# A decoder trunk's middle: combining expert outputs, norm, turn and value products in one loop over token tiles

## The reference

```python
h = h + s5_mixer(rmsnorm(h, norm_mix[0]), ...)          # layer 0
h = h + hier_moe(rmsnorm(h, norm_ffn[0]), ...)          # 2 of 32 experts for each token
# in hier_moe, last step: out[tok] += gate_k * y[tok, k] for k = 0, 1
k, v = split(rmsnorm(h, norm_kv) @ w_kv + b_kv)         # 256 + 256 columns
q = rmsnorm(h, norm_mix[1]) @ w_q + b_q                 # 1024 columns
h = h + attention(q, k, v) @ w_o + b_o                  # window 128, meta tokens, sinks
h = h + hier_moe(rmsnorm(h, norm_ffn[1]), ...)          # layer 1
out = rmsnorm(h, norm_final)[:, 16:]
# rmsnorm(x, g) = x / sqrt(mean(x * x) + 1e-6) * g
```

## Time and profile before

| | us |
|---|---|
| median of 3 runs | 2242.67 (2241.44 to 2243.80) |
| the profiled execution: its own time | 2243.16 |
| its span, first to last instruction | 2241.4 |
| PE busy / DVE / ACT / POOL in the span | 1985.4 / 1586.7 / 1244.6 / 369.5 |
| mean granted TensorE clock | 0.941 of full speed |

### The profile page before, as it was taken

The page is one execution under the profiler, slowest core; times in us unless marked ns, Lnnn a source line. Parts: engine busy times, 40 slices in busy tenths (PEclk is TensorE's granted clock), DMA queues, the critical chain, the costliest instruction groups (busy, mean ns, idle before and its releaser), DMA issues. The chain is left out here.

```text
span 2241.4 us, 31742 instructions
## 1 busy us (share of the span) xinstructions
PE 1985.4 (89%) x10658; PEld 1572.3 (70%) x10658; DVE 1586.7 (71%) x1770; ACT 1244.6 (56%) x1521; POOL 369.5 (16%) x684
## 2 busy tenths in 40 slices
PE   4859999659999999999189999998599999999991
PEld 3558777548888888887178766666388888888880
DVE  8995221558888888887642276663688888888885
ACT  6524110437777777776120065554277777777772
POOL 2000000302211112221224000002022212112214
PEclk9979999879999999999579999999699999999995
DMA  3265100639999999996521020005299999999985
GB/s 98 36 60 176 63 1 1 248 113 365 381 375 371 367 373 374 377 376 253 189 67 38 10 86 1 1 1 198 103 343 360 360 375 385 378 384 387 383 315 235
DMA packets 136045, 504.69 MB, mean 225 GB/s; under 512 B 38466, under 2 KB 68498, under 8 KB 84754
## 3 DMA queue, kind: packets, MB, share of 16 engines
q1 hardware_dynamic: 116258, 468.85, 57.4%
q0 software_dynamic: 18432, 33.86, 4.0%
q10 hardware_dynamic: 1280, 0.98, 0.3%
HBM read 488.47 MB, written 47.32 MB: 239 GB/s over the span
## 5 line engine op out<-in xcount | busy, mean ns | idle before, releaser
L1406 DVE TENSOR_TENSOR moe_lo<-moe_raw,moe_hi 128x2048 fp32r<-128x2048 f32 x378 | 861.0, 2292 | 118.4 <-ACT moe_hi L1191 114.1
L1191 ACT CAST moe_hi<-moe_raw 128x2048 fp32r<-128x2048 f32 x374 | 714.2, 1915 | 153.5 <-PE moe_ps_g L1546 74.9
L1544 PE MATMUL moe_ps_g<-moe_hi,moe_x_hi 128*128 128x512 f32 x512 | 211.6, 413 | 7.2 <-DVE moe_x_lo L1411 4.7
L1544 PE MATMUL moe_ps_y<-moe_hi,moe_h_hi 128*128 128x512 f32 x512 | 209.0, 408 | 3.7 <-DVE moe_h_lo L1422 3.7
L1545 PE MATMUL moe_ps_g<-moe_hi,moe_x_lo 128*128 128x512 f32 x512 | 205.8, 402 | 0.0
L1546 PE MATMUL moe_ps_g<-moe_lo,moe_x_hi 128*128 128x512 f32 x512 | 205.3, 401 | 0.0
L1545 PE MATMUL moe_ps_y<-moe_hi,moe_h_lo 128*128 128x512 f32 x512 | 204.2, 399 | 0.0
L1546 PE MATMUL moe_ps_y<-moe_lo,moe_h_hi 128*128 128x512 f32 x512 | 203.9, 398 | 0.0
L1546 PE MATMUL moe_ps_u<-moe_lo,moe_x_hi 128*128 128x512 f32 x512 | 203.0, 396 | 0.0
L1544 PE MATMUL moe_ps_u<-moe_hi,moe_x_hi 128*128 128x512 f32 x512 | 202.8, 396 | 0.0
L1545 PE MATMUL moe_ps_u<-moe_hi,moe_x_lo 128*128 128x512 f32 x512 | 202.8, 396 | 0.0
(11 more groups left out here) (406 smaller groups left out, 3699.1 us busy)
## 6 DMA issues: line engine op xcount, KB each, us to landing
moe_raw<-moe_w_gate SPq DMA_DIRECT2D x128, 1024.0 KB, 7.3
moe_raw<-moe_w_up SPq DMA_DIRECT2D x128, 1024.0 KB, 8.0
moe_raw<-moe_w_down SPq DMA_DIRECT2D x128, 1024.0 KB, 7.3
moe_raw<-y_dram SPq DMA_DIRECT2D x16, 1024.0 KB, 11.6
mix_r<-ssm_w_glu SPq DMA_DIRECT2D x16, 512.0 KB, 5.2
xn_dram<-moe_work SPq DMA_DIRECT2D x16, 512.0 KB, 7.4
mix_r<-x SPq DMA_DIRECT2D x8, 512.0 KB, 5.4
mix_r<-h_dram SPq DMA_DIRECT2D x16, 256.0 KB, 11.6
```

Source lines behind the costliest of these rows:

```text
L1191: A.copy(hi[:, slot(number, k), :], raw[:, k, :]).then_inc(hi_done, 1)
L1406: V.tensor_tensor(lo[:, slot, :], raw[:, k, :], hi[:, slot, :].bitcast(F32), ALU.subtract).then_inc(lo_done, 1)
L1544: T.matmul(out, x_h, w_h, start=first, stop=False)
```

## The change

**In `phase_moe`, layer 0.** The tiles' loads and the combine leave the phase, but for the first four loads (`load_pair`), which SyncE still issues at its end. They go to a buffer `yc` of its own with four places, which lies over the expert phase's `hi` and the first slot of `lo`. The order of tiles is now `TILE_ORDER`: the meta tile first, then 0 to 7. The four K/V weight blocks are loaded here, as soon as `raw` slot 3 of the last expert has been split, into `w_raw` (over `raw` slots 2 and 3); block numbers 0 and 1 are now V, 2 and 3 K. VectorE multiplies them by the gain and later subtracts the `hi` part in place (`w_lo` has the address of `w_raw`); ScalarE makes the `hi` parts (`w_hi`, over `raw` slots 4 and 5) ahead of the last `store_y`.

**In `phase_project`.** One loop over the tiles does everything up to V. On VectorE, trip j combines tile j, writes 1/rms of tile j-1 onto a diagonal (`prj_scale` = identity times the column `rstd`), takes the `lo` part of tile j-2 and the V result of tile j-3. TensorE's `turn` multiplies the tile itself by that diagonal (float32 `matmul`), which normalises and turns at once, so `prj_xn` is gone; behind `turn(j)` stands the V product of tile j-1. K and Q blocks follow as before, with four weight slots in place of three and two; a Q block is loaded when the products of the block four before it are done. The three bias loads and the Q gain are issued by ScalarE at the head of its list. Ahead of the first turn, TensorE multiplies the identity by itself 20 times.

```diff
+W_KV = 4
+N_YC = 4
+RAW_AT = 229344 - 6 * 8192
+TILE_ORDER = (XT,) + tuple(range(XT))
...
+def kv_columns(t, n):
+
+    half = DC // W_KV
+    at = (n + half) % W_KV * P
+    return t["w_kv"].rearrange("(p c) f -> p c f", c=DC)[:, :, at:at + P]
...
+def load_pair(sp, t, j):
+
+    i = TILE_ORDER[j]
+    n = tile_rows(i)
+    sp.dma_start(t["yc"][0:n, j % N_YC],
+                 t["y_dram0"][2 * i * P:2 * (i * P + n), :].rearrange("(p k) d -> p k d", k=2)
+                 ).then_inc(t["yc_in"][j % N_YC], 16)
...
+            else:
+
+                sp.dma_start(g_kv[:, :], t["norm_kv"].rearrange("(p c) -> p c", c=DC)).then_inc(wkv_in, 16)
+                sp.wait_ge(lo_done, n_q * 6 + (-2))
+                for n in range(W_KV):
+                    sp.dma_start(t["w_raw"][:, n], kv_columns(t, n)).then_inc(wkv_in, 16)
...
-            for i in range(NT):
+            if not last_layer:
+                for j in range(N_YC):
+                    load_pair(sp, t, j)
+            for i in range(NT if last_layer else 0):
                 if i >= NB:
                     sp.wait_ge(h_new, 2 * (i - NB + 1))
...
             store_y(n_q - 2, n_q * 6)
+            if not last_layer:
+                for n in range(W_KV):
+                    act.wait_ge(gained, n + 1)
+                    A.copy(t["w_hi"][:, n], t["w_raw"][:, n]).then_inc(wkv_hi, 1)
             store_y(n_q - 1, n_q * 6 + 2)
...
+            if not last_layer:
+                dve.wait_ge(wkv_in, 16 * (W_KV + 1))
+                for n in range(W_KV):
+                    V.tensor_tensor(t["w_raw"][:, n], t["w_raw"][:, n], g_kv[:, :].unsqueeze(2).to_broadcast([P, DC, P]),
+                                    ALU.mult).then_inc(gained, 1)
+                for n in range(W_KV):
+                    dve.wait_ge(wkv_hi, n + 1)
+                    V.tensor_tensor(t["w_lo"][:, n], t["w_raw"][:, n], t["w_hi"][:, n].bitcast(F32),
+                                    ALU.subtract).then_inc(wkv_lo, 1)
...
+                    load_pair(sp, t, j)
+            for i in range(NT if last_layer else 0):
...
+            for j in range(N_YC, NT):
+                sp.wait_ge(h_new, 2 * (j - N_YC + 1))
+                load_pair(sp, t, j)
...
+            for n in range(Q0, NC):
+                sp.wait_ge(acc_done, jobs_to(n - W_KV))
+                sp.dma_start(w_raw[:, n % W_KV], w_q[:, :, (n - Q0) * P:(n - Q0 + 1) * P]).then_inc(w_in[n % W_KV], 16)
...
+            for j, i in enumerate(TILE_ORDER):
...
+            pool.wait_ge(gain_in, 16)
             pool.wait_ge(bo_in, 16)
-            pool.wait_ge(xn_done, NT)
-            for n in range(3, NP):
-                gain(n)
-                if n >= V_P:
-                    i = n - V_P
-                    nc.gpsimd.tensor_tensor(h[:, i, :], h[:, i, :], sq[:, :], ALU.add).then_inc(bo_added, 1)
...
+            A = nc.scalar
+            A.dma_start(bv[:, :], t["b_kv"][KV:].partition_broadcast(P)).then_inc(bias_in, 16)
+            A.dma_start(bk[:, :], t["b_kv"][0:KV].rearrange("(c p) -> p c", p=P),
+                        allow_slow_non_contiguous=True).then_inc(bias_in, 16)
+            A.dma_start(bq[:, :], t["b_q"][0].rearrange("(c p) -> p c", p=P),
+                        allow_slow_non_contiguous=True).then_inc(bias_in, 16)
+            A.dma_start(g_q[:, :], t["norm_mix"][1].rearrange("(p c) -> p c", c=DC)).then_inc(gain_in, 16)
...
+            for j in range(NT):
+                squares(j)
+                if j >= 1:
+                    hi_part(j - 1)
+            hi_part(NT - 1)
...
+            def combine(j):
+                i = TILE_ORDER[j]
+                n = tile_rows(i)
+                dve.wait_ge(yc_in[j % N_YC], 16 * (j // N_YC + 1))
+                for k in range(2):
+                    V.scalar_tensor_tensor(h[0:n, i, :], yc[0:n, j % N_YC, k, :], gates[0:n, k, i:i + 1],
+                                           h[0:n, i, :], ALU.mult, ALU.add).then_inc(h_new, 1)
+                    dve.wait_ge(h_new, 2 * j + k + 1)
+
+            def set_scale(j):
+                i = TILE_ORDER[j]
+                n = tile_rows(i)
+                dve.wait_ge(rstd_done, j + 1)
+                if j >= 2:
+                    dve.wait_ge(xt_mm, j - 1)
+                V.tensor_scalar(scale[0:n, j % 2, 0:n], ident[0:n, 0:n], rstd[0:n, i:i + 1], None,
+                                ALU.mult).then_inc(scale_set, 1)
...
+            for j in range(NT + 3):
+                if j < NT:
+                    combine(j)
+                if 1 <= j <= NT:
+                    set_scale(j - 1)
+                if 2 <= j <= NT + 1:
+                    lo_part(j - 2)
+                if j == 3:
+                    dve.wait_ge(bias_in, 48)
+                if j >= 3:
+                    values(j - 3)
+            k = NT
...
+            def turn(j):
+                i = TILE_ORDER[j]
+                n = tile_rows(i)
+                pe.wait_ge(scale_set, j + 1)
+                if j >= 2:
+                    pe.wait_ge(xt_lo, j - 1)
+                for c in range(DC):
+                    last = T.matmul(ps_x[:, j % 2, c * P:c * P + n],
+                                    h[0:n, i, :].rearrange("p (m c) -> p c m", c=DC)[:, c, :],
+                                    scale[0:n, j % 2, 0:n], start=True, stop=True)
+                last.then_inc(xt_mm, 1)
+
...
+            def value_product(j):
+                pe.wait_ge(xt_lo, j + 1)
+                i = TILE_ORDER[j]
+                product(j, 0, i * P, tile_rows(i))
             pe.wait_ge(ident_step, 2)
+            for _ in range(20):
+                T.matmul(acc[:, 3, 0:P], ident[:], ident[:], start=True, stop=True)
+            for j in range(NT):
+                turn(j)
+                if j >= 1:
+                    value_product(j - 1)
...
-                pe.wait_ge(xn_done, i + 1)
-                if i >= 2:
-                    pe.wait_ge(xt_lo, i - 1)
-                for c in range(DC):
-                    last = T.transpose(ps_x[:, i % 2, c * P:c * P + n],
-                                       xn[0:n, i % 2, :].rearrange("p (m c) -> p c m", c=DC)[:, c, :],
-                                       ident[0:n, 0:n])
-                last.then_inc(xt_mm, 1)
```

More of the change, by code:

```diff
@@ L871, in phase_moe @@
         sem = semaphore_source(nc, ctx, f"moe{layer}_")
+        hi, lo = (sb(x, [P, 3, KC * F], F32R) for x in ("hi", "lo"))
         ident = sb("ident", [P, P])
@@ L919, in phase_moe @@
         n_more = sb("n_more", [1, 1], I32)
-        raw = sb("raw", [P, 6, KC * F])
-        hi, lo = (sb(x, [P, 3, KC * F], F32R) for x in ("hi", "lo"))
+        raw = nc.alloc_sbuf_tensor_at(f"moe{layer}_raw", [P, 6, KC * F], F32, offset=RAW_AT)
+        g_kv = sb("g_kv", [P, DC])
         gi = sb("gi", [P, 1], I32)
@@ L954, in phase_moe @@
                              "ht_mm", "ht_hi", "ht_lo", "y_done", "y_out"))
-        yc_in = [sem(f"yc_in{b}") for b in range(NB)]
+        if last_layer:
+            yc_in = [sem(f"yc_in{b}") for b in range(NB)]
+        wkv_in, gained, wkv_hi, wkv_lo = (sem(x) for x in ("wkv_in", "gained", "wkv_hi", "wkv_lo"))
         y_free, h_new, fin_sq, fin_rstd, fin_done, out_done = (
@@ L1659, in jobs, with jobs_to @@
         def jobs(n):
-            if n < K_P:
+            if n < K0:
+                return [(i * P, tile_rows(i)) for i in TILE_ORDER] if n == K0 - 1 else []
+            if n < Q0:
                 return [(0, 512), (512, 512), (XT * P, N_META)]
-            if n < V_P:
-                return [(i * P, tile_rows(i)) for i in range(NT)] if n == V_P - 1 else []
             return [(0, 512), (512, 512)]
-        def jobs_before(n):
-            return sum(len(jobs(m)) for m in range(n))
+        def jobs_to(n):
+            return sum(len(jobs(m)) for m in range(max(n + 1, K0)))
         block = ctx.enter_context(nc.Block())
@@ new lines, in hi_part @@
+            def hi_part(j):
+                i = TILE_ORDER[j]
+                n = tile_rows(i)
+                act.wait_ge(xt_mm, j + 1)
+                A.copy(x_hi[:, :, i * P:i * P + n],
+                       ps_x[:, j % 2, :].rearrange("p (c m) -> p c m", c=DC)[:, :, 0:n]).then_inc(xt_hi, 1)
+            for j in range(NT):
[3 more added lines that the diff above has]
+            hi_part(NT - 1)
+            for n in range(Q0, NC):
+                act.wait_ge(gained, n - Q0 + 1)
+                A.copy(w_hi[:, n % W_KV], w_raw[:, n % W_KV]).then_inc(w_hi_done, 1)
@@ L1787, in _ @@
-            k = 0
-            for n in range(NP):
-                ahead = n + 1 < NP and n != V_P - 1
-                if ahead:
+            dve.wait_ge(ident_step, 2)
+            for j in range(NT + 3):
[9 more added lines that the diff above has]
+                    values(j - 3)
@@ L1791, in _ @@
+            k = NT
+            for n in range(K0, NC):
+                if Q0 <= n + 1 < NC:
                     split_w(n + 1)
@@ new lines, in product @@
+            def product(k, n, at, m):
```

(26 more changed lines are left out.)

164 lines of the change are left out of this document (51 added, 113 removed).

## The result

The changed kernel takes 2214.56 us (median of 4 runs, 2213.56 to 2215.1), the kernel before beside it 2243.24 (2241.44 to 2245.32): ratio 0.9871, 95% interval 0.9857 to 0.9885. The direction was right; the gain is 28.7 us where 43.7 were forecast, and the time lies 1.6 us above the range. The profiled execution took 2213.56 us, its span is 2211.8.

A forecast was written before the change was run, and what follows sets the result against it. It took the combine as bound by VectorE, the norm part by a chain through four engines, the products by TensorE. Phase start 1073.8 + 53.2 to the last V + 27.6 K + 89.1 Q = 1243.7, before 1287.3: 2199.5 us, range 2190 to 2213.

The forecast's parts named there:

- the full turn: Loop over tiles: a float32 product by the diagonal takes 16 rows of 0.12, 1.96 us at full clock, eight times.
- The old turns took 1.97 at half clock, so nothing is lost there: Loop over tiles: the new turn, 1.96 us at full clock, costs no more than the old one.
- TensorE sets the pace of the loop: Loop over tiles: TensorE's trip is 4.80 us, VectorE's 4.54, so TensorE bounds it by 0.26 us.
- The phase's end at 1.34 us: Between `phase_moe` and `phase_project`: ending the phase costs 1.34 us, behind 1.7 us of load issues.
- The lock at the last scatter: End of layer 0's experts: VectorE's subtractions delay GpSimd's copy and scatter by 1.0 us, bounds 0 and 2.5.
- ScalarE's four small loads, 4.8 us: Start of `phase_project`: ScalarE issues four small loads before its first square, 4.8 us, bounds 0 and 8.
- The 20 identity products: Ahead of the first turn: they end 5.6 to 10.5 us into the phase, delaying nothing or under half a us.
- K and Q: Behind the V products: K takes 27.6 us, Q 89.1, at full clock and without a gap.
- Rival (1): Loop over tiles: GpSimd's 1/rms waits behind combines, VectorE sets the pace, 5.4 us a trip, +5, 2204 us; 12%.
- Rival (2): Loop over tiles: matmuls stay at half clock, 74 us in place of 41.3, +31, 2231 us; 8%.
- Rival (3): Loop over tiles: tiles run one after the other, 12.0 us each, +55, 2255 us; 4%.
- Rival (4): Whole change: nothing gained, since the time before the end was covered by something else, 2243 us; 2%.

The follow-up runs named there:

- experiment 1: Changed kernel with each turn reading 128 contiguous features of `h`, weights and gains reordered alike: 2199.12 us.
- experiment 5: Changed kernel with operands of the full tiles' turning products swapped, so the diagonal is loaded and `h` streams past it: 2214.18 us.
- experiment 9: Changed kernel with turns reading `h` at a step of 8 bytes in place of 32, weights keeping their order: 2199.09 us.
- experiment 2: Changed kernel with VectorE writing the normalised tile and TensorE transposing it, in place of products with the diagonal: 2194.82 us.
- experiment 4: Changed kernel with one tile load ahead of the phase's end in place of four: 2220.66 us.
- experiment 6: Changed kernel with GpSimd waiting, behind its last scatter, for the load of tile 0 before the phase's end: 2219.36 us.
- experiment 10: Kernel of experiment 2 with the first tile's combine moved ahead of the phase's end: 2195.89 us.
- experiment 11: Kernel of experiment 1 with the first tile's combine moved ahead of the phase's end: 2201.49 us.
- experiment 12: Kernel of experiment 10 with `b_k`, `b_q` and `g_q` loaded by SyncE later: 2196.14 us.
- experiment 3: Changed kernel without the 20 identity products: 2215.23 us.

## Why the prediction was right in direction and short in size

- **The failed step** is a term of the sum, the full turn, in the sentence "16 rows of 0.12 = 1.96 us at full clock". The 0.12 came from products with the identity, where both operands are contiguous; the turn reads `h` with a step of 32 bytes, and a row takes 0.24 (experiments 1, 5 and 9). 8 × 1.86 = 14.9 us, nearly the whole miss of 15.1; without the step the time is 2199.12, against a forecast of 2199.5. That it fits so closely is in part luck: in that profile the phase's end is dearer by 2.4 us and K and Q by 2.0, but the way from the phase's first row to the last V result is 50.1 us in place of 53.2, and the unchanged part ahead was 2.8 shorter than in the profile the forecast started from. V results 6.66 us apart also lie beyond the 5.5 that the prediction named as a sign of being wrong. The same mistake carried "The old turns took 1.97 at half clock, so nothing is lost there": those were transposes, one row each, which the step doesn't slow (experiment 2).
- **TensorE sets the pace of the loop:** right, and by 2 us a trip instead of 0.26. With the step gone it is right as said: 4.61 measured against 4.80, VectorE close behind with 4.4.
- **The phase's end at 1.34 us:** wrong. It was read where VectorE ended last and GpSimd's drain of 5.56 us lay beneath the combine. From the last scatter's row the end takes 6.40 us in place of 1.7 + 1.34 = 3.0 (experiments 4 and 6). The 1.7 us of load issues lie beside the drain. As the last scatter came no later than before, 6.40 stand against 4.04: the +2.4 of the table.
- **The lock at the last scatter:** right in kind, and that no delay is seen is luck. The last scatter's last row stands 13.56 us behind the experts' last `lo` part (1066.29 against 1052.73), 13.55 before. Beside VectorE's weight work GpSimd's last copy took 1.01 us (0.18 before), and the start of the scatter ahead of it 1.81 (1.00 before). That scatter ended 7.55 us behind the `lo` part in place of 5.05, so ScalarE's last store now waits for it, and not for TensorE. But TensorE's last expert products had the full clock, where it stood at 0.55 before: they ended 6.8 us behind the `lo` part in place of 8.3. That hides the rest. Some 0.8 us at the store and 0.8 at the copy are what the lock cost, an estimate from these rows. Why the clock was up is not shown. The clock of that stretch, then the rows:

```profile
1053.70:1057.20 3.50, 3.50 (x15) 2.86 (x16) 3.50 (x4) 2.45 (x3) 3.27 (x3) 1.00 0.00 0
```

```profile
1055.88 1.81 POOL L1163 DMA_INDIRECT y_dram<-moe_y,moe_si  x1 [0.15 <-issue]
...
1060.36 1.01 ACT L1245 COPY moe_y<-moe_ps_y 128x1024 f32<-128x1024 f32 x1 [1.32 <-POOL moe_unit L1167]
1061.53 1.01 POOL L1147 COPY moe_si<-moe_idx_out 128x1 int32 x1 [1.25 <-ACT moe_y L1245]
```

- **ScalarE's four small loads, 4.8 us:** too dear; 0.41 + 0.46 + 0.49 + 0.60 = 2.0 us on its queue, and off the path there, since the squares wait for the combine until 1076.2. They matter only once that wait is gone (experiments 10 to 12).
- **The 20 identity products "delay nothing, or by under half a us":** the last of them ended 1.35 us behind the first diagonal (1080.94 against 1079.59). In the profile without them the way from the phase's first row to the last V result is 67.1 us in place of 68.7; in the medians there is nothing of it (experiment 3).
- **K and Q:** right, 118.05 against 117.6, with no wait for weights.
- **The last step of the sum:** from 2199.6 the prediction takes off 0.5 and says 2199.5; its own sum gives 2199.1. Nothing hangs on it.
- **Rival (1), the lock of VectorE and GpSimd in the loop:** GpSimd's `pow` took 1.45 to 1.62 us in the first three trips and 0.55 after; VectorE waited for it 1.6 us in all. It is real at the start and does not set the pace. **Rival (2)**, half clock: it fell, 0.99 in the loop. **Rival (3)**, one tile after the other: it fell, V results come every 6.66 us, not every 12. **Rival (4)**, nothing gained: it fell with the 28.7 us.
